# A streaming encoder step on one core: attention steps in one run on TensorE, regrouped by kv head

## What is computed

```python
xn = rmsnorm(x, p['norm1_g'])
proj = xn @ p['w_in']            # q, k, v, sc_b, sc_c, sc_h, cf_a, cf_gate, gate_pre
y_attn = attend(q, k, v, sinks) @ p['w_attn_out']
y_sc = (sc_b * conv3(sc_c * sc_h)) @ p['w_sc_out']
y_cf = silu(layernorm(conv31(cf_a * sigmoid(cf_gate)))) @ p['w_cf_out']
x = x + (g_attn * y_attn + g_sc * y_sc + g_cf * y_cf) @ p['w_o']
h = conv3(rmsnorm(x, p['norm2_g']) @ p['w_up'])
x = x + (silu(hg) * hu) @ p['w_down']
```

## Time and profile before

| | before |
|---|---|
| median of three runs | 2459.11 us |
| the profiled execution, its time | 2460.99 us |
| its span in the trace | 2459.7 us |
| TensorE busy | 2390.1 us (97%) |
| VectorE busy | 1616.4 us (66%) |
| ScalarE busy | 891.3 us (36%) |
| granted TensorE clock, mean | 0.992 of full |
| attention stretch of layer 0 | about 100 to 270 us |

### The profile page before, as it was taken

How to read it: one execution, slowest core, us unless ns; L and a number is a source line. 1 busy time by engine, 2 the same in 40 slices (tenths; PEclk the granted TensorE clock), 3 DMA queues, 4 the chain that set the end, 5 groups by cost and what they waited for, 6 DMA issues and landing times.

```text
span 2459.7 us, 41837 instructions
## 1 busy us (share of the span) xinstructions
PE 2390.1 (97%) x17698; PEld 2342.4 (95%) x17698; DVE 1616.4 (66%) x2393; ACT 891.3 (36%) x1704; POOL 41.5 (2%) x73
## 2 busy tenths in 40 slices
PE   7999999999999999999999999999999999999997
PEld 6988899999999999999998889999999999999996
DVE  6577698895535664645764777988864356556366
ACT  4355322223523432423434562222244234234243
POOL 2000000000000000000010000000000000000000
PEclk9999999999999999999999999999999999999998
DMA  5311222222332222222242112222223322222222
GB/s 195 93 44 52 65 78 86 79 78 78 96 103 88 81 78 81 83 78 86 90 141 69 52 45 75 85 78 86 78 78 95 100 86 79 85 78 85 79 78 93
DMA packets 58284, 206.30 MB, mean 84 GB/s; under 512 B 8494, under 2 KB 8590, under 8 KB 57838
## 3 DMA queue, kind: packets, MB, share of 16 engines
q1 hardware_dynamic: 54704, 191.56, 24.0%
q0 software_dynamic: 3392, 12.05, 1.7%
HBM read 192.09 MB, written 8.50 MB: 82 GB/s over the span
## 4 chain that ended last, share of the span: by engine, by line
PE 89%; DVE 6%; ACT 2%; issue 2%; DMA 0%; SPq 0%; DVEq 0%; ACTq 0%
PE ps L386 86%; DVE cf_acc L1016 1%; PE ps L430 1%; DVE w_lo L825 1%; PE ps L443 1%; PE ps L462 1%; ACT w_hi L574 1%; PE ps L466 0%; DVE xn_hi_lo L873 0%; PE ps L398 0%; ACT scratch L657 0%; ACT L651 0%; ACT L601 0%; DVE scratch L869 0%; PE ps L448 0%
## 5 line engine op out<-in xcount | busy, mean ns | idle before, releaser
L386 PE MATMUL ps<-xn_hi_lo,w_hi 128*128 128x304 f32 (+1 forms) x7552 | 1358.5, 302 | 20.6 <-DVE w_lo L825 12.8
L386 PEld LDWEIGHTS ps<-xn_hi_lo,w_hi 128*128 128x128 f32 x7552 | 1122.7, 189 | 39.2 <-issue 27.3
L386 PE MATMUL ps<-xn_hi_lo,w_lo 128*128 128x304 f32 x3776 | 821.9, 299 | 0.0
L825 DVE TENSOR_TENSOR w_lo<-raw,w_hi 128x1024 fp32r<-128x1024 f32 x348 | 426.2, 1225 | 543.2 <-ACT w_hi L574 543.2
L574 ACT ACTIVATE w_hi<-raw 128x1024 fp32r<-128x1024 f32 x348 | 369.0, 1060 | 1121.2 <-PE ps L386 1120.7
L386 PEld LDWEIGHTS ps<-xn_hi_lo,w_lo 128*128 128x128 f32 x3776 | 609.2, 189 | 0.0
L386 PE MATMUL ps<-branch_hi_lo,w_hi 128*128 128x304 f32 (+1 forms) x2944 | 523.1, 300 | 3.8 <-DVE branch_hi_lo L1161 1.6
L386 PEld LDWEIGHTS ps<-branch_hi_lo,w_hi 128*128 128x128 f32 x2944 | 436.2, 188 | 6.7 <-DVE branch_hi_lo L1161 2.1
L1016 DVE SCALAR_TENSOR_TENSOR cf_acc<-glu,vec,cf_acc 128x622 f32<-128x622 f32 x480 | 382.8, 861 | 0.0
L386 PE MATMUL ps<-branch_hi_lo,w_lo 128*128 128x304 f32 x1472 | 318.9, 298 | 0.0
L386 PEld LDWEIGHTS ps<-branch_hi_lo,w_lo 128*128 128x128 f32 x1472 | 236.1, 188 | 0.0
(11 more groups left out here) (123 smaller groups left out, 1293.2 us busy)
## 6 DMA issues: line engine op xcount, KB each, us to landing
raw<-in_weights SPq DMA_DIRECT2D x348, 512.0 KB, 3.4
spill<-x_q_merged POOLq DMA_DIRECT2D x2, 2368.0 KB, 9.4
x_q_merged<-spill POOLq DMA_DIRECT2D x16, 296.0 KB, 3.2
x_q_merged<-in_xt SPq DMA_DIRECT2D x4, 592.0 KB, 8.7
out_y<-x_q_merged SPq DMA_DIRECT2D x8, 296.0 KB, 2.2
scratch<-scratch SPq DMA_DIRECT2D x72, 18.5 KB
scratch<-scratch SPq DMA_DIRECT2D x8, 132.0 KB, 2.3
con<-in_consts SPq DMA_DIRECT2D x1, 592.0 KB, 12.1
```

Source lines behind the costliest of these rows:

```text
L386: last = nc.tensor.matmul(to[:, t0:t1], a[:, w % 2, wk], both[:, part, k, t0:t1], start=(k == 0 and j == 0), stop=(k == nk - 1 and j == 2))
L825: V.tensor_tensor(wl[:, w % 2, :], raw[:, w % 2, :], f(wh[:, w % 2, :]), ALU.subtract).then_inc(lo_done, 1)
```

## The change

The attention starts at panel 7 (`N_SHADE`), the sixth query panel, in place of panel 10. The steps are no longer six units apart but 34/5: step s is at u = 4 + floor(34 s / 5), where u now counts from panel 7. In a step s TensorE does, with no unit between, values(s-3), scores(s) and turn(s-2). ScalarE: slot 1 copies(s-2), slot 2 exps(s), slot 3 outputs_hi(s-3). VectorE: slot 0 divided(s-1) and then maxima(s), slots 1 and 2 taps, slot 5 outputs_lo(s-3). Items go kv head by kv head: ten chunks of head 0, then ten of head 1, so scores(0) needs four rotated queries and scores(10) all eight. Queries 5 to 7 are copied and rotated within the steps. The values' results move to free columns of the scores' banks, so values also waits for exps of the item before the present scores (`p_done`) and for `ol_done`. The turned queries lie in `cf_acc` instead of `scratch`. The first tap is an Identity on ScalarE with the tap's weight as scale.

```diff
-SHADE, SLOT = 10, 6
+N_SHADE = N_Q + 5
+SHADE = KT * (N_OA + 1 - N_SHADE)
+STEP = {4 + 34 * s // 5: s for s in range(ITEMS + 3)}
+def step_at(u):
+    for k in range(7):
+        if u - k in STEP:
+            return STEP[u - k], k
+    return -1, 0
...
+    def rq(s):
+        return turning[:, TOK * s:TOK * (s + 1)]
+    def outputs_ps(e):
+        return PS[:, 4 + e, 384:512]
...
         def scores(l, i):
-            c, v = divmod(i, N_KV)
+            v, c = divmod(i, CHUNKS)
             if i == 0:
-                pe.wait_ge(q_rot, l * KT + KT)
+                pe.wait_ge(q_rot, l * KT + 4)
...
+            if i == CHUNKS:
+                pe.wait_ge(q_rot, l * KT + KT)
...
         def turn(l, i):
             pe.wait_ge(pn_done, g + 1)
             if g:
-                pe.wait_ge(ol_done, g)
+                pe.wait_ge(pt1_done, g)
...
             if n2:
+                if rests(l, i):
+                    pe.wait_ge(pt2_done, rests(l, i))
...
         def values(l, i):
+            pe.wait_ge(p_done, l * ITEMS + min(i + 3, ITEMS))
+            if g:
+                pe.wait_ge(ol_done, g)
...
         def attention_at(l, u):
-            i, k = divmod(u - SHADE, SLOT)
-            if k == 0 and 0 <= i < ITEMS:
-                scores(l, i)
-            if k == 1 and 1 <= i <= ITEMS:
-                turn(l, i - 1)
-            if k == 3 and 1 <= i <= ITEMS:
-                values(l, i - 1)
+            s, k = step_at(u)
+            if k == 0:
+                if 3 <= s:
+                    values(l, s - 3)
+                if 0 <= s < ITEMS:
+                    scores(l, s)
+                if 2 <= s < ITEMS + 2:
+                    turn(l, s - 2)
...
-            for m in range(1, KT):
+            for m in range(1, N_SHADE - N_Q):
...
                     if m == 0:
-                        pe.wait_ge(ol_done, l * ITEMS + (ITEMS - 1 if k < 4 else ITEMS))
+                        pe.wait_ge(ol_done, (l + 1) * ITEMS)
...
ScalarE:
             def outputs_hi(i):
                 act.wait_ge(o_done, l * ITEMS + i + 1)
+                act.wait_ge(ds_done, l * ITEMS + min(i + 4, ITEMS))
...
+            def tap_one(m):
+                tile_emptied(act, (l, N_CF + 2 * m + 1))
+                nc.scalar.activation(acc[:, m, :], G[:, m, 0:CF_OUT], ACT.Identity, bias=0.0, scale=col(l, "cfw", m * CF_K)) \
+                    .then_inc(tap_first, 1)
...
             def attention_at(u):
-                i, k = divmod(u - SHADE, SLOT)
-                if k == 1 and 1 <= i <= ITEMS:
-                    copy_first(i - 1)
-                    copy_rest(i - 1)
-                if k == 2 and 0 <= i < ITEMS:
-                    exps(i)
-                if k == 4 and 1 <= i <= ITEMS:
-                    outputs_hi(i - 1)
+                s, k = step_at(u)
+                if k == 1 and 2 <= s < ITEMS + 2:
+                    copies(s - 2)
+                if k == 2 and 0 <= s < ITEMS:
+                    exps(s)
+                if k == 3 and 3 <= s:
+                    outputs_hi(s - 3)
...
+            for u in range(SHADE):
+                n, k = N_SHADE + u // KT, u % KT
+                if k == 0 and u:
+                    high(W + n + 1)
+                    if n <= N_CF:
+                        query(n - 1 - N_Q)
+                    elif (n - N_CF) % 2:
+                        if n - N_CF >= 5:
+                            tile_emptied(act, (l, n - 4))
+                        gate(l, n - 1, (n - N_CF) // 2 % 2, 0.0)
+                if n > N_CF and k == 5 and (n - N_CF) % 2 == 0:
+                    tap_one((n - N_CF) // 2 - 1)
                 attention_at(u)
...
VectorE:
             def outputs_lo(i):
                 dve.wait_ge(oh_done, l * ITEMS + i + 1)
+                dve.wait_ge(p_done, l * ITEMS + min(i + 4, ITEMS))
...
             def attention_at(u):
+                s, k = step_at(u)
+                if k == 0 and 1 <= s <= ITEMS:
+                    divided(s - 1)
+                if k == 0 and 0 <= s < ITEMS:
+                    maxima(s)
+                if u > KT * (N_CF + 4 - N_SHADE) and (k == 1 or (k == 2 and s % 2)):
                     taps(1)
-                if k == 4 and 0 <= i < ITEMS:
-                    divided(i)
-                if k == 5 and 1 <= i <= ITEMS:
-                    outputs_lo(i - 1)
+                if k == 5 and 3 <= s:
+                    outputs_lo(s - 3)
...
+            for u in range(SHADE):
+                n, k = N_SHADE + u // KT, u % KT
+                if k == 0 and u:
+                    low(W + n + 1)
+                    if n <= N_CF:
+                        rotation(n - 2 - N_Q)
+                    elif (n - N_CF) % 2 == 0:
+                        glu((n - N_CF) // 2 - 1)
+                if n == N_CF and k == 4:
+                    rotation(KT - 1)
                 attention_at(u)
```

More of the change, by code:

```diff
@@ L54 @@
 O_KD, O_VV = 0, 1440
[L55 removed]
+O_RT, O_NT = 5856, 6448
 O_SQ, O_SS = 3488, 4732
@@ L245, in encoder @@
     g_zero = sem("g_zero")
-    tap = [sem(f"tap{g}") for g in range(4)]
+    tap_first, tap = sem("tap_first"), [sem(f"tap{g}") for g in range(4)]
     mg_done, mg_hi, mg_lo = sem("mg_done"), sem("mg_hi"), sem("mg_lo")
@@ L279, in swap @@
         def swap(s):
-            a, b = slot(O_QR, TOK, s), slot(O_SW, TOK, s)
+            a, b = rq(s), swapped(s)
             for h in (0, HEAD_DIM):
@@ L502, in _ @@
                             at = (4 + 2 * j) * BANK + 128 * b
-                            last = nc.tensor.transpose(flat[0:n, at:at + 128], slot(O_QR, TOK, 1)[:, t0:t0 + n], ident)
+                            last = nc.tensor.transpose(flat[0:n, at:at + 128], rq(1)[:, t0:t0 + n], ident)
                         last.then_inc(vt_ps, 1)
                 panel(l, N_Q + m, XN)
-            for u in range(2 * KT * KT):
+            for u in range(SHADE):
                 attention_at(l, u)
[L509 to L512, removed]
+                unit(l, N_SHADE + u // KT, u % KT, XN)
             for m in range(KT):
@@ L642, in _ @@
                     act.wait_ge(sw_in[m % 2], swaps(l, m - 2))
[L643 to L644 removed]
+                nc.scalar.activation(rq(m % 2), ps((l, N_Q + m)), ACT.Copy).then_inc(out[USES[(l, N_Q + m)][0]], 1)
             def exps(i):
[L647 removed]
+                g, b, nk = l * ITEMS + i, i % 2, chunk_span(i % CHUNKS)[2]
                 act.wait_ge(ds_done, g + 1)
@@ L878, in key_value @@
                 dve.wait_ge(panel_done, W + j + 1)
-                V.tensor_tensor(slot(O_QR, TOK, j), ps((l, j)), view(O_RT, TOK), ALU.mult).then_inc(out[USES[(l, j)][0]], 1)
+                V.tensor_tensor(rq(j), ps((l, j)), view(O_RT, TOK), ALU.mult).then_inc(out[USES[(l, j)][0]], 1)
             rsqrt((l, "n1"), TOK, O_RT, l * 3 + 1)
@@ L897, in _ @@
             dve.wait_ge(sin_signed, 2)
-            k, ksw = slot(O_QR, TOK, 0), slot(O_SW, TOK, 0)
+            k, ksw = rq(0), swapped(0)
             dve.wait_ge(sw_in[0], swaps(l, -1))
@@ L923, in value_tiles @@
                 last.then_inc(vv_done, 1)
-            for m in range(KT):
+            for m in range(N_SHADE - N_Q):
                 low(W + N_Q + m + 2)
@@ L1006, in taps @@
                 for at in range(taps_begun, taps_begun + n):
[L1007 to L1009 removed]
+                    g, k = divmod(at, CF_K - 1)
                     for t in (2 * g, 2 * g + 1):
[L1011 removed]
                         if k == 0:
[L1013 removed]
+                            dve.wait_ge(tap_first, l * KT + t + 1)
                         else:
[L1015 to L1017 removed]
+                            dve.wait_ge(tap[g], l * (2 * CF_K - 2) + 2 * k - 1 + t - 2 * g)
+                        V.scalar_tensor_tensor(acc[:, t, :], G[:, t, k + 1:k + 1 + CF_OUT], col(l, "cfw", t * CF_K + k + 1),
+                                               acc[:, t, :], ALU.mult, ALU.add).then_inc(tap[g], 1)
                 taps_begun += n
[L1020 to L1025 removed]
+            for u in range(SHADE):
+                n, k = N_SHADE + u // KT, u % KT
[7 more added lines that the diff above has]
+                    rotation(KT - 1)
                 attention_at(u)
@@ L1080, in tile_sum @@
                 if m % 2 or m == 1:
-                    dve.wait_ge(tap[m // 2], (l + 1) * (2 * CF_K))
+                    dve.wait_ge(tap[m // 2], (l + 1) * (2 * CF_K - 2))
                 if m == 1:
@@ L1113, in _ @@
                     merge(m, N_OS + p, 0)
-                if p < 2:
-                    taps(min(3, 4 * CF_K - taps_begun))
+                if p < 3:
+                    taps(min(3, 4 * CF_K - 4 - taps_begun))
                 work, tiles = plan.get(p, (None, ()))
```

125 lines of the change are left out of this document (49 added, 76 removed).

## The result

The changed kernel takes 2483.86 us (2482.73 to 2486.27, four runs) against 2459.41 us of the kernel before in the same comparison: the ratio is 1.0101, 95% interval 1.0083 to 1.0118. It is slower, by 24.4 us. The forecast was 2471 us, slower by 12.3; the direction and the places were right, the forecast was half of the size.

The account below looks back on a forecast made before the run. TensorE, busy for 97% of the span, was taken as the bound. Stalls of 24.05 us a layer against 14.5 (+19.1 over two layers), minus 6.8 for switches, gave 2459.1 + 12.3 = 2471.4 us; range 2460 to 2484.

Parts of the forecast that it names:

- Runs: TensorE's three attention groups run together: 0.20 us saved per step in 17 steps a layer, 6.8 us in all.
- Stalls: TensorE in the attention stretch, mostly values waiting for outputs_lo: 24.05 us a layer against 14.5 before.
- start: First scores, four units into panel 7, wait for rotation(3) behind w_lo: 1.5 us a layer.
- s=3: Step 3: outputs_lo(0) stands behind low, rotations, divided and maxima on VectorE: stall of 2.4 us.
- s=7: Step 7, panel boundary five units after its run, with GLU ahead of outputs_lo: stall of 2.1 us.
- s=14: Step 14, panel boundary five units after its run, with GLU ahead of outputs_lo: stall of 2.1 us.
- s=10: Step 10, boundary at the run itself, w_lo and GLU ahead of divided and maxima: stall of 0.2 us.
- about 8: Sign of being right: about 8 TensorE waits per layer charged to outputs_lo before the values matmuls.
- The first tap, the turned queries' place, v_twice: Tap moved to ScalarE, turned queries in cf_acc, GpSimd's copies of the values: each taken to cost no time.
- Tables: ScalarE's table loads at gates: 1.28 us a switch; the skill's 2.66 us would add 17 us over two layers.
- The sum: Whole kernel: +19.1 us of stalls over two layers, minus 6.8 saved by runs, +12.3 us; chance 0.70.
- the third: Rival 3: VectorE falls behind, lag carried into the next maxima, 1.0 us in six steps a layer: 2483; chance 0.10.

Follow-up runs that it names:

- e7: e4 with one unit between values and scores, all else the same: 2433.53 us, ratio 0.9892.
- e4: The changed kernel with panel-boundary work in slots 1 to 3 (ScalarE) or 0 to 5 (VectorE) put behind that step's outputs_hi or outputs_lo: 2423.06 us.
- e2: The changed kernel with the first tap of each tile back on VectorE: 2483.16 us, ratio 1.0088.
- e3: The changed kernel with outputs_lo at slot 2 of a step in place of slot 5: 2465.02 us, ratio 1.0013.
- e6: e4 with rotation(3) ahead of the w_lo of panel 8 and rotation(5) behind the maxima of step 2: 2418.39 us, ratio 0.9830.
- e5: The changed kernel with 4 to 6 extra matmuls into unused PSUM columns ahead of the values of seven stalled steps: 2465.38 us, ratio 1.0018.
- e8: The kernel before, six units a step, with boundary work in a step's slots put behind its outputs_hi or outputs_lo (or maxima): 2428.88 us, ratio 0.9874.

## Why the prediction was wrong

Step by step:

- **Runs.** Forecast R = 2.67 us for a full run. Measured, by the timeline of the changed kernel between the values of two stall-free steps of seven units:

```profile
160.40 0.66 PE L493 MATMUL ps<-scratch 128*64 128x128 f32 x8
...
168.75 0.66 PE L493 MATMUL ps<-scratch 128*64 128x128 f32 x8
```

  168.75 - 160.40 = 8.35 us, less 7 x 0.816, is 2.64 us. Right. The reason given for the saving was read too simply, though. The rows have a late start of 0.09 us where TensorE enters the small shapes and a slow first block of 0.11 where it leaves them, which is 0.20 for the pair and not for each switch, and e7 measures one such pair, 0.21. Between small shapes nothing is lost that the rows show: in e7's timeline a unit starts 0.38 us after the last values (158.47 to 158.85), and in e4's the scores do as well (158.77 to 159.15). Counted either way a run saves about 0.2 us, so the number held.
- **Stalls.** Forecast 24.05 us a layer, measured 24.4 and 24.1. (What a gap loses beyond its idle time is 0.16 us at the transposes but 0.08 at scores and values, so the old waits are nearer 14.3 us a layer than 14.5.) Step by step (forecast, measured from start to start, layer 0): start 1.5, 1.54; s=2 0.65, 0.69; s=3 2.4, 1.96; s=4 3.05, 3.14; s=7 2.1, 2.16; s=11 2.6, 2.8; s=14 2.1, 2.5; s=17 2.1, 2.0; s=18 3.05, 3.19; s=20 1.4, 1.41. The wait of 0.2 at s=10 did not come, and the tap on ScalarE is in the 2.5 of s=14 (2.1 in e2). All names of waiter and releaser were right; the waits for outputs_lo are 13 a layer, as in the forecast's own list of steps, and not the "about 8" of its signs. e3, e4 and e6 took the waits away by order alone, which shows the mechanism.
- **The first tap, the turned queries' place, v_twice**: forecast at nothing. The tap cost 0.7 us in layer 0 and nothing in layer 1 (e2); for the other two only the absence of any wait for them speaks.
- **Tables.** Each load took 1.28 us with nothing behind it: 114.63 + 1.28 = 115.91, and the gate starts at 115.92. The 2.66 us that the Trainium skill (ScalarE: Activation LUTs, "What ACT_TABLE_LOAD costs") gives for a switch is again not seen here.
- **The sum** is what failed. "Over two layers +19.1, minus 6.8: +12.3 us" has no term for TensorE's clock. The forecast priced a stall as idle time alone, although the timeline of before had a fall behind its 2.68 us wait. Eleven falls instead of three are eight more; at up to 1.7 us they are up to 13.6 us, at the 1.6 us that e5's timeline shows 12.8. Measured are 24.4 - 12.3 = 12.1 us. e5 takes ten falls away, leaves the stalls' ends where they were and gains 18.5 us.

Of the rivals, none was right: the third had the sign of the error and nearly its size (2483), but its mechanism, VectorE falling behind, is refuted by e3, e4 and e8, in which the same VectorE work fits with no stalls. That the range reached to 2484, just above the 2483.86 measured, came from that rival and from no thought of the clock; that the time lies inside it is luck.

## What to carry to other kernels

Where every engine runs a list in order, the place of periodic work against a dependency chain can decide more than the distance between steps, as it did here: put work that has time (here eight units) behind what the next engine waits for, before spacing the steps out. A step distance that does not divide the panel length moves the boundary through all slots of a step, and so finds each bad order. When a stall of TensorE is priced, look in the trace at the matmuls behind it, not only at the gap, and add what they lose. Take that from several executions: the number of falls was not the same in each.

## What the runs showed of the hardware that was not expected

- A stall of 1.9 to 3.2 us cost 1.6 us more when the clock fell behind it. Of the 14 such stalls after the change ten were followed by 3.4 us at 1.2 GHz, of the two of 1.5 us one; the two of 1.4 us and the shorter ones were not. Of two stalls of the same length (2.16 us after s=7 in both layers) one was followed by a fall and one was not. In the kernel before, the six longer waits of TensorE for the exps (1.8 us idle, 1.9 from start to start) had two falls behind them and the two of 2.7 us one, so length alone does not tell.
- Extra matmuls of no use in such stalls pay: e5, 18.5 us from 33 of them a layer. The one fall left in it stands behind the wait of 1.5 us at the start of layer 1, which was not filled.
- A float32 matmul of 256 columns on the full array took 0.44 us, in two instructions, while the kernel's own matmuls of 304 columns, on operands rounded to fp32r, are one instruction each and follow one another after 0.14 us.
